# Moving the value products of the sliding-window heads ahead of the transposes in a hybrid attention trunk

## The reference

```
for each block of 128 queries:
    compressed: softmax(q ck^T + bias) over 63 pooled keys, times cv     (o_c)
    selected:   softmax over the top 8 blocks of 64 keys, causal         (o_s)
    sliding:    softmax(q k_win^T + bias) over the last 512 keys, causal (o_w)
    o = gate0 * o_c + gate1 * o_s + gate2 * o_w
```

## Time and profile before

| | |
|---|---|
| median of 3 runs | 2567.41 us (2564.76 to 2568.99) |
| the profiled execution's span | 2567.2 us |
| PE busy | 2490.1 us (97%) |
| DVE busy | 1777.3 us (69%) |
| POOL busy | 1204.3 us (47%) |
| ACT busy | 1109.4 us (43%) |
| window part, about | 1354 to 1608 us of the span |

### The profile page before, as it was taken

The page is one execution under the profiler, slowest core; times in us unless marked ns, Lnnn a source line. Parts: engine busy times, 40 slices in busy tenths (PEclk is TensorE's granted clock), DMA queues, the critical chain, the costliest instruction groups (busy, mean ns, idle before and its releaser), DMA issues.

```text
span 2567.2 us, 38264 instructions
## 1 busy us (share of the span) xinstructions
PE 2490.1 (97%) x14136; PEld 2006.5 (78%) x14136; DVE 1777.3 (69%) x2859; ACT 1109.4 (43%) x2142; POOL 1204.3 (47%) x939
## 2 busy tenths in 40 slices
PE   8999999999999999999999999999999999999999
PEld 5777666888887778877877777788788888787887
DVE  6654755466777999964037777676547677899993
ACT  4526544243334334323126666566524333433430
POOL 5362676234445444443315777546423454544441
PEclk8999999999999999999999999999999999999999
DMA  4010002223443544303231112353322343364431
GB/s 172 33 50 33 1 2 111 82 86 136 158 158 107 213 155 174 131 34 131 87 97 57 55 55 75 88 150 87 116 78 86 138 162 152 107 224 165 157 128 66
DMA packets 91199, 275.78 MB, mean 107 GB/s; under 512 B 9879, under 2 KB 39191, under 8 KB 76359
## 3 DMA queue, kind: packets, MB, share of 16 engines
q1 hardware_dynamic: 87464, 255.18, 29.1%
q10 hardware_dynamic: 3552, 18.18, 1.8%
HBM read 197.50 MB, written 73.86 MB: 106 GB/s over the span
## 4 chain that ended last, share of the span: by engine, by line
PE 84%; DVE 9%; issue 3%; POOL 2%; ACT 1%; DMA 1%; DVEq 0%; SPq 0%; ACTq 0%; POOLq 0%
PE ps L1718 21%; PE ps L1723 20%; PE ps L1722 20%; PE ps L2285 5%; PE ps L2301 5%; PE ps L2260 2%; DVE RL L925 1%; POOL MX L1517 1%; PE ps L2275 1%; PE ps L2276 1%; PE ps L1947 1%; DVE U_lo L959 1%; PE ps L1976 1%; DVE H L989 1%; PE ps L1961 1%
## 5 line engine op out<-in xcount | busy, mean ns | idle before, releaser
L1718 PE MATMUL ps<-U_hi,RH 128*128 128x512 f32 x912 | 356.6, 391 | 12.3 <-DVE H L978 4.8
L1723 PE MATMUL ps<-U_hi,RL 128*128 128x512 f32 x912 | 355.6, 390 | 0.0
L1722 PE MATMUL ps<-U_lo,RH 128*128 128x512 f32 x912 | 355.5, 390 | 0.0
L1113 POOL TENSOR_TENSOR RL<-RAW,RH 128x512 fp32r<-128x512 f32 x112 | 155.6, 1389 | 393.8 <-ACT RH L817 393.8
L817 ACT ACTIVATE RH<-RAW 128x512 fp32r<-128x512 f32 x280 | 175.5, 628 | 289.9 <-PE ps L1723 282.7
L1718 PE MATMUL ps<-U_hi,W_hi 128*128 128x512 f32 (+2 forms) x656 | 262.3, 400 | 12.3 <-DVE U_lo L2995 11.0
L1718 PE MATMUL ps<-SH,RH 128*128 128x512 f32 x656 | 256.0, 390 | 9.9 <-DVE H L978 5.7
L1723 PE MATMUL ps<-U_hi,W_lo 128*128 128x512 f32 (+2 forms) x656 | 258.5, 394 | 0.0
L1722 PE MATMUL ps<-U_lo,W_hi 128*128 128x512 f32 (+2 forms) x656 | 258.4, 394 | 0.0
L1723 PE MATMUL ps<-SH,RL 128*128 128x512 f32 x656 | 255.3, 389 | 0.0
L1722 PE MATMUL ps<-SL,RH 128*128 128x512 f32 x656 | 255.2, 389 | 0.0
(11 more groups left out here) (403 smaller groups left out, 6087.2 us busy)
## 6 DMA issues: line engine op xcount, KB each, us to landing
W_raw<-in_pieces SPq DMA_DIRECT2D x30, 1024.0 KB, 5.2
RAW<-in_pieces SPq DMA_DIRECT2D x28, 1024.0 KB, 4.8
RAW<-in_pieces SPq DMA_DIRECT2D x56, 512.0 KB, 8.0
hid_d<-HOA SPq DMA_DIRECT2D x24, 1024.0 KB, 3.9
hid_d<-HOB SPq DMA_DIRECT2D x24, 768.0 KB, 5.4
RHA<-hid_d SPq DMA_DIRECT2D x12, 1024.0 KB, 5.1
RHB<-hid_d SPq DMA_DIRECT2D x12, 768.0 KB, 6.6
U_rawh<-hid_d SPq DMA_DIRECT2D x12, 768.0 KB, 4.8
```

Source lines behind the costliest of these rows:

```text
L1113: G_.tensor_tensor(ring(RL[i], n), quarter(n, (B22, B11)[i - 5]), ring(RH[i], n).bitcast(F32), ALU.subtract).then_inc(u_lop.sem, 1)
L1718: m = mm(o, a_hi, b_hi, start=first, stop=False, skip_group_check=again)
L1722: mm(o, a_hi, b_lo, start=False, stop=False, skip_group_check=again)
L1723: return mm(o, a_lo, b_hi, start=False, stop=last, skip_group_check=again)
```

## The change

On PE, for steps 1 to 64, the value products of the step before are issued right after the scores and the compressed products, in front of the other transposes, the compressed scores and both heads' transposes. For the steps of the selected branch the products stay between the two heads' transposes. On ACT, `window_out` moves from between the two exponentials to before the copy of the first head's transposes. `SEQ` is as it was, since the order of the chunks in banks 4 to 6 does not change.

```diff
@@ PE @@
                 if cell(s, 10) is not None:
                     cmp_weigh(cell(s, 10))
+                if 0 < s <= N_BR:
+                    weigh_p(s - 1)
                 for g in imp_of(s, 42):
                     imp_turn(g, 0)
                     imp_turn(g, 1)
@@
                 if s < N_STEP:
                     turn_p(2 * s)
-                if s:
+                if s > N_BR:
                     weigh_p(s - 1)
                 if s < N_STEP:
                     turn_p(2 * s + 1)
@@ ACT @@
                 if s == 2:
                     ck_high()
+                if s % 4 == 0 and 0 < s <= N_BR:
+                    window_out(s // 4 - 1)
                 if s < N_STEP:
                     copy_p(2 * s)
                 for t in scored_in(s):
                     expo(2 * t)
-                if s % 4 == 0 and 0 < s <= N_BR:
-                    window_out(s // 4 - 1)
                 for t in scored_in(s):
                     expo(2 * t + 1)
```

## The result

The change made the kernel slower. The medians are 2615.47 us after (4 runs, 2611.38 to 2616.61) against 2568.2 us before (4 runs, 2564.76 to 2570.32). The ratio is 1.0181, with a 95% interval of 1.0167 to 1.0196. That is outside the predicted range: the side was right, the size was too small.

What follows compares the result with a forecast made beforehand. PE was taken to bound the kernel, busy 246.94 of 254.00 us. Terms of 9.6 + 13.0 + 2.6 + 6.9 - 1.1 = 31.0 us on 2567.2 gave 2598 us, with a range of 2576 to 2610.

Steps and rivals of the forecast that it cites:

- B: Place 1 and key steps: products now stand ahead of the chain to the next scores; 8.7 and 4.3, together 13.0 us.
- key steps: Steps 2, 6, 7, 10, 11: key pieces' chains start later, like place 1's query chain; 0.5 to 1.24 each, 4.3 us.
- A: Mainly places 0 and 4: products wait for DVE's late copy of the second head; 10.7 minus 1.1, 9.6 us.
- D: Places 5 to 6: later exponentials delay DVE's reciprocal and compressed addition, so second-head transposes wait; 6.9 us.
- C: Places 0, 4 and 2: transposes wait for one of three PSUM banks to be freed; 2.6 us.
- joined gains: Each step's two transpose runs, now directly joined, save about 0.14 us, lost where a wait follows.
- E: Gains kept: only place 5 has no such wait right behind; 8 x 0.14, minus 1.1 us.
- the removed switch: Joining both heads' transpose runs saves about 0.14 us per step, 9.0 us over 64 steps if nothing is late.
- upper bound: Each late step also pushes DVE's next copy: 31.0 + 8 = 39 us for the whole change.
- Switches win: Rival: waits vanish in slack and the saved 0.14 stays in all steps; 2558 us, 5%.
- Only the chains: Rival: DVE gets ahead, so copies and reciprocals are in time; 12.6 us, about 2580, 20%.
- Every cover lost: Rival: products no longer cover anything, mean 0.97 us per step over 64 steps; 62 us, 2629, 7%.

Runs made afterwards that it cites:

- e8: The changed kernel with ACT's window copy back at its old place between the two exponentials; 2616.4 us, 1.0196 of the kernel before.
- e9: The changed kernel with 12 extra filling transposes at place 1, seven times; 2610.41 us, 1.0173 of the kernel before.
- e1: Kernel before with the products early only at place 1 (steps 1, 9, ..., 57), ACT as before; 2583.31 us, ratio 1.0052.
- e3: Kernel before with the products early only at place 5 (step number 5 modulo 8); 2572.44 us, ratio 1.0023.
- e10: e3 with ACT's exponentials at place 5 no longer behind its copies; 2566.15 us, 0.9994 of the kernel before.
- e4: Kernel before with the products early only at places 3 and 7, from step 15 on; 2568.99 us, ratio 1.0002.
- e5: Kernel before with the products behind both heads' transposes at odd places, between them as before at even ones; 2564.68 us, ratio 0.9987.
- e12: e5 with DVE's bias of the second head ahead of the query's second half at place 1; 2564.18 us, 0.9985 of the kernel before.
- e11: e2 with DVE's copy of the second head ahead of the compressed sum at places 3 and 7; 2577.82 us, 1.0037 of the kernel before.
- e2: Kernel before with the products early only at places 0 and 4 (steps 4, 8, ..., 64); 2583.71 us, ratio 1.0067.
- e6: Kernel before with the window part's products behind all other pieces, directly in front of both heads' transposes; 2581.18 us, ratio 1.0061.
- e7: e1 with 12 extra transposes at place 1, behind the first head's, where PE would idle; 2577.49 us, 1.0045 of the kernel before.

## Why the prediction was right in direction and short in size

The steps of after less those of before, by the forecast's terms (from step 0 to step 65, in us). "Clock" is what a step has beyond its like without a fall of the clock (the same step in e8 or e9, or the same place in another period), and is taken out of the other rows. It is an estimate:

| term | forecast | measured |
|---|---|---|
| place 1 (B) | 8.7 | 8.5 |
| key steps 2, 6, 7, 10, 11 (B, with A at 6 and 10) | 5.5 | 5.1 |
| place 6 and its likes (D) | 6.9 | 6.5 |
| places 0 and 4 (A and C, with the joined gains that they took back) | 12.1 | 16.4 |
| place 2 (C) | 0.5 | 1.8 |
| places 3, 5, 7 and step 57 | -2.8 | -1.7 |
| clock | not in the sum | 5.2 |

**B was right.** The chain took 3.50 us in both traces, and e1 shows 8.5 us from place 1 alone. The key steps came out as worked, step 7 at 1.10 and step 11 at 1.09 for 1.24 each.

**D was right**, in size (0.94 to 0.96 for 0.8 in six periods, less than that in the two others) and in mechanism: e3 alone makes it, and e10 takes it away by changing only ACT's order.

**E and the removed switch were right.** Where no wait follows, a step is 0.11 to 0.17 shorter against the 0.14 read from the earlier trace rows. Five kernels show it (after, e3, e4, e5, e12). The Trainium skill, page TensorEngine Tiling (Array Packing), section Key Properties, says that a change of the tiling mode drains TensorE. The saving is in line with that, but no run tells a drain from another cost of starting or ending a run.

**The step that failed inside the sum is C, the banks.** The forecast had 1.9 us for it at places 0 and 4 and 0.1 at each place 2. The starts of PE's rows in after part it from A. From the first transposes to the next scores PE takes 1.76 us at each place 4 for 1.35 before, 0.41 more where the forecast had 0.17. At place 0 it takes 1.85 (1.76 at step 56) for 1.36 to 1.66, which is 0.19 to 0.46 more and 2.2 in seven steps, where it had 0.5. So C is 5.5 for 1.9 there, most of the 4.3 that the table's row is short. Each place 2 costs 0.34 to 0.39, which makes 1.8 for 0.5. e11 shows the same 1.85 and 1.76 with the copy nearly in time.

At step 36 one can see what was missing. The bias ends 0.95 us after the first transposes start, as read. The five transposes behind it start 0.14 later (1521.81 to 1521.95) and take 0.67 to the next scores, as a run of five does. The forecast let them start at once and gave them 0.44 + 0.11, the rate inside a run. (Its own terms make 1.50, not 1.52.) At place 0, where the forecast had 0.5 in all, PE waits 0.42 us for the bias at six of seven steps.

**A was right in sum, and partly by luck.** From the scores' start to the next piece of work (in after the products) PE takes 9.0 us more in after than before: 4.1 at places 0 (0.18 to 1.05) and 4.9 at places 4 (0.29 to 1.00). The forecast had 5.4 + 3.3 - 1.1, and 1.7 of joined gains taken back, 9.3. Two errors of it cancel. PE issues a little after what it waits for: products at 1518.44 behind a copy that ends at 1518.29, 0.15 late, as behind the bias (0.14) and the addition (1529.25 to 1529.40). The sum took issue as instant; as an estimate, 15 late copies x 0.15 are 2.3 us. Against them stands a gain that I had put too low. The small DVE products that take 1.05 us beside POOL's gating in three periods of before take 0.25, 0.22 and 0.25 in after (the one that answers to the earlier trace rows starts at 1533.80, POOL's gating at 1532.98, 1.04 long). That is 2.4 us where I had taken 1.1. Those of steps 16, 20, 28, 36 and 48, which took 0.33 to 0.50 before, take 0.17 in after, another 1.3 that I had not counted.

The rest of the waits' 5.5 is small: steps 60, 61 and 64 cost some 0.9 more than forecast, 1.1 of the joined gains did not come, and B and D were 1.0 too high.

**The step that failed outside the sum is the clock.** "Whatever makes PE wait adds to the time" held, but it adds more than its own length. I had priced idle time at its length only, having read a clock of 1.00 in the earlier trace rows, where PE had idled 7 us in all. The profiled execution lost about 5.2 us to it, e1 8.3. Not every wait costs it: in e2, with 8.3 us of waits for the copy, 1.2 us the longest, the clock is 1.00 over the stage, and so it is in e3 and e6. Without the clock the stage would be 36.5 us longer, within the forecast's upper bound of 39. Here is the first such place of after that stands apart, step 34:

```profile
1507.00:1509.00 2.00, 0.40 (x6) 0.20 (x4) 1.74 (x4) 1.52 (x5) 0.00 (x0) 1.00 0.33 74
1509.00:1511.00 2.00, 1.95 (x18) 1.03 (x16) 2.00 (x7) 0.70 (x2) 1.58 (x2) 0.89 1.00 287
1511.00:1513.00 2.00, 2.00 (x12) 1.67 (x10) 0.34 (x3) 0.45 (x1) 1.95 (x3) 0.50 0.46 164
```

The runs of one kernel also differ in this. The profiled execution of after was the fastest of four: its span is 2609.3 at a mean granted clock of 0.990, the others' 2613.1 to 2614.8 at 0.987 to 0.990. So the medians differ by 47.3 us where the profiled spans differ by 42.1. The other 5.2 us lie in executions without a trace; a lower clock would fit two of the three, but it is not shown.

**The account.** Forecast 31.0, the waits' shortfall 5.5 (36.5 in the stage without the clock), the clock 5.2, the rest of the span 0.4, and 5.2 that no trace shows: 47.3. The parts tried alone come near it: 8.8 for e1 (17.1 less 8.3 of clock), 15.6, 4.4 and 1.1 for e2, e3 and e4, together 29.9. With 5.1 and 1.8 for the key steps and place 2, which no run tried alone and which are read in after itself, that is 36.8 against 36.5. So the waits add up in the profiled executions; the 5.2 without a trace stay open.

**The rivals.** "Switches win" fell: the gain is real, but e5 keeps 3 us of it and e4 nothing, since it stays only where nothing behind is just in time. "Only the chains" fell: e2 costs 15.6 us and not 2, and e3 4.4 and not -1.1. DVE's idle time did not let it get ahead, since it idles in waits for PE and ACT. "Every cover lost" fell: places 3, 5 and 7 cost nothing. The upper end of the range, 2610, came from adding half of A and D again, which did not happen. It had no term for the clock, and C as small as it was.

Left open is which of several like idle times costs clock. Place 1 to 2 of after idles 1.60 us at step 26 (1473.86) and at step 34 (1508.80). The clock stays at 1.00 behind the first and falls to 0.50 behind the second, though the rows behind both (1509.00 above and this one) are alike in PE's work and the DMA's:

```profile
1474.00:1476.00 2.00, 1.95 (x18) 0.90 (x18) 2.00 (x7) 0.76 (x2) 1.53 (x2) 1.00 0.98 279
```

## What to carry to other kernels

Before moving work forward in an in-order queue, list what it covered on every other engine, place by place: a copy, a chain, an exponential, a bank. Here each move uncovered one of them, and moving the products backwards at odd places, the only direction in which covers grow, gained 0.13%. Where a wait falls inside a run of transposes, price what stands behind it as a run of its own. On a saturated TensorE, allow for an idle stretch to cost more than its length, and look at the granted clock just behind it.

## What the runs showed of the hardware

- A TensorE idle time of 1.6 us between otherwise full stretches can be followed by some microseconds at a granted clock of 0.50 (1.2 GHz). In e1 four of five idle times of 1.60 us were followed by a loss of 1.5 to 1.6 us each, as much as the idle time itself, and the fifth by none. In e9 the clock also fell (step 44) behind 20 us in which no idle time was longer than 0.47 us.
- With twelve 128x128 float32 transposes in that idle time the clock stayed at 1.00 over the stage (e7). They took 1.34 us (1457.20 to 1458.54), 0.11 each. The Trainium skill, page TensorE: Matmul & The Clock Gate, section Part 4: PE-mode transpose, says that the full clock doesn't engage for transposes in TensorE's transpose mode. By that rule, if it holds for these, e7 would have been as slow as e1. The trace does not agree: the clock was 1.00 throughout those stretches.
- The small DVE product of 0.17 us ends when POOL's gating ends if it starts during it, however late. In the kernel before, eight of them start inside a gating (steps 16 to 40 and 48), and all end 0.02 to 0.06 us behind it. The DVE reciprocal just ahead of the product takes its plain 0.20 inside the gating (after, 1462.49, in a gating from 1461.91 to 1462.96). In e3, at step 39, the gating starts at 1505.88 and takes 1.05, and the product starts at 1506.71 and takes 0.24. In e5 the product starts at 1503.14, 0.10 before the gating, and takes its plain 0.17. So a shift between DVE and POOL either way releases it: steps 24, 32 and 40 are 0.23 to 0.27 shorter in e3, e5, e10 and e12.
